# Expert outputs scattered by token inside the expert loop, and the gather-and-combine phase merged into it

## The reference, cut to what matters

```python
top_v, top_i = lax.top_k(logit_e, TOP_K)              # 2 of the 8 experts of the token's group
gate = jax.nn.softmax(top_v, axis=-1) * p_grp
...
def expert_block(args):                               # a block of rows that share an expert
    xb, e = args
    g, u = jnp.split(xb @ w_up[e], 2, axis=-1)
    return (jax.nn.silu(g) * u) @ w_down[e]
...
y = y[dest] * gate.reshape(-1)[order][:, None]
return jax.ops.segment_sum(y, tok_sorted, num_segments=n_tok)
...
x = x + mod[:, 5] * f                                 # then rms_norm_2(x, final_g)
```

## Time and the profile before

| | us |
|---|---|
| median of 3 runs (lowest, highest) | 2867.06 (2861.56, 2873.09) |
| the profiled execution, its own time | 2889.24 |
| its span in the trace | 2887.4 |
| PE busy | 2759.5 (96%) |
| DVE busy | 1506.3 (52%) |
| ACT busy | 777.0 (27%) |
| POOL busy | 79.0 (3%) |
| mean granted clock of PE | 0.982 |

### The profile page before, as it was taken

How to read it: one execution, slowest core, us unless ns; L and a number is a source line. 1 busy time by engine, 2 the same in 40 slices (tenths; PEclk the granted TensorE clock), 3 DMA queues, 4 the chain that set the end, 5 groups by cost and what they waited for, 6 DMA issues and landing times. The chain is left out here.

```text
span 2887.4 us, 44114 instructions
## 1 busy us (share of the span) xinstructions
PE 2759.5 (96%) x18251; PEld 1644.2 (57%) x18251; DVE 1506.3 (52%) x2115; ACT 777.0 (27%) x1444; POOL 79.0 (3%) x106
## 2 busy tenths in 40 slices
PE   8999889999999999999999989999998899999985
PEld 4444554444444444444454445656564899999974
DVE  7886676566666668773642008856765111111103
ACT  2111771111111115412100016756423121112111
POOL 0000000000000000000000000000000000000022
PEclk9999999999999999999999999999999899999997
DMA  3022842111111127763231000022202999999992
GB/s 143 31 73 40 264 175 73 44 44 44 44 44 44 44 67 280 265 245 111 71 90 44 8 11 1 1 59 88 75 7 75 375 402 406 409 410 405 405 359 79
DMA packets 82614, 422.65 MB, mean 146 GB/s; under 512 B 13504, under 2 KB 23232, under 8 KB 66496
## 3 DMA queue, kind: packets, MB, share of 16 engines
q1 hardware_dynamic: 58528, 362.29, 34.1%
q10 hardware_dynamic: 15664, 41.95, 4.0%
q0 software_dynamic: 8304, 16.79, 1.8%
HBM read 393.07 MB, written 51.38 MB: 154 GB/s over the span
## 5 line engine op out<-in xcount | busy, mean ns | idle before, releaser
L3605 PE MATMUL ex_up_ps<-big,ex_xT 128*32 128x128 f32 x3072 | 349.1, 274 | 0.0
L3603 PE MATMUL ex_up_ps<-big,ex_xT 128*32 128x384 f32 x3072 | 344.8, 490 | 0.7 <-ACT ex_xT L3690 0.6
L3605 PEld LDWEIGHTS ex_up_ps<-big,ex_xT 128*32 128x32 f32 x3072 | 334.3, 110 | 0.6
L1758 PE MATMUL ffn_ps<-h,V 128*128 128x512 f32 x504 | 219.7, 592 | 0.0
L2217 PE MATMUL ffn_ps<-big,V 128*128 128x512 f32 x484 | 211.3, 597 | 3.7 <-DVE V L2472 1.4
L3603 PE MATMUL ex_y_ps<-ex_wd,ex_hT 128*32 128x384 f32 x1536 | 180.9, 493 | 5.1 <-issue 4.3
L296 DVE TENSOR_SCALAR_CACHE_REDUCE h<-ad_s_ps 128x1280 f32<-128x1280 f32 x64 | 92.9, 1489 | 172.7 <-PE ad_s_ps L205 172.7
L3605 PE MATMUL ex_y_ps<-ex_wd,ex_hT 128*32 128x128 f32 x1536 | 178.8, 276 | 3.0 <-issue 2.9
L3605 PEld LDWEIGHTS ex_y_ps<-ex_wd,ex_hT 128*32 128x32 f32 x1536 | 169.0, 111 | 7.2 <-issue 6.5
L1758 PEld LDWEIGHTS ffn_ps<-h,V 128*128 128x128 f32 x504 | 95.8, 190 | 120.5 <-issue 120.5
L2217 PEld LDWEIGHTS ffn_ps<-big,V 128*128 128x128 f32 x484 | 92.2, 191 | 120.4 <-issue 114.5
(11 more groups left out here) (603 smaller groups left out, 4799.0 us busy)
## 6 DMA issues: line engine op xcount, KB each, us to landing
big<-in_w_eup SPq DMA_DIRECT2D x64, 2048.0 KB, 20.9
ex_wd<-in_w_edown SPq DMA_DIRECT2D x32, 2048.0 KB, 20.7
V<-in_w_down SPq DMA_DIRECT2D x35, 704.0 KB, 5.6
dn_tail<-in_w_mod ACTq DMA_DIRECT2D x48, 512.0 KB, 5.4
fm_up<-in_w_up SPq DMA_DIRECT2D x22, 1028.0 KB, 4.9
y_dram<-in_cos SPq DMA_DIRECT2D x1, 21504.0 KB, 71.5
y_dram<-big ACTq DMA_DIRECT2D x32, 288.0 KB
dn_tail<-in_w_in SPq DMA_DIRECT2D x17, 512.0 KB, 4.6
```

The costliest lines, as they stand in the source:

```text
L1758: mm = nc.tensor.matmul(bank(i, j), wj[:, k, :], bj[:, k, :], start=(k == 0), stop=(k == 3))
L3603: nc.tensor.matmul(o[32 * g:32 * g + 32, 0:W], rows(g), w[:, 0:W], start=first, stop=last)
L3605: mm = nc.tensor.matmul(o[BR:P, g * P:(g + 1) * P], rows(g), w[:, W:BANK], start=first and g == 0, stop=last and g == GR - 1)
```

## The change

Outputs are no longer stored by block and gathered by token. Each block is scattered to a table of 2048 rows in token order while the loop runs, and read back by plain loads. Of a token's two assignments, the one with the lower expert number goes to row `token`, the other to `1024 + token`; `swapped` remembers where that exchanges the gates.

1. The fill of `y_dram` and its wait are gone.
2. route: `early` and `late` are replaced by one table `rows` (slot to row of the new `y_dram`; an empty slot gets 2048, which is out of bounds and not written). The router adds `swapped` and `code`, and `count` has a third entry. The row ring of h2 stays in SBUF and is used again (`rows`), and `std` with it.
3. experts, ACT: `store_y` becomes `move_y`, three DMAs from SBUF to SBUF that bring the last 256 columns of 32 rows each beside the first 768.
4. experts, POOL: `scatter(i, u)`, an indirect DMA of 96 rows of 4 KB to `y_dram`, and `free(i, u)`, which waits until it has landed and releases the buffer for `keep_y`.
5. the loops are nested, three groups of nine trips, each group with an `If` of its own (not on POOL, whose loop is one of 26 trips).
6. combine is part of experts, with no barrier. DVE computes the gates before its first block. SP loads the lower-expert rows `f0` when pair 15's first block has landed, in the order 4, 0, 5, 1, 6, 2, 7, 3, and the others, `f1`, when the last block has. Tiles 0 to 3 are summed on PE as before; for tiles 4 to 7 ACT scales f0 and DVE adds the residual from the row ring (`added`). The last multiplication of an even tile is split: ACT by the reciprocal root (`leveled`), then GpSimd by the gain. Odd tiles stay on DVE.

```diff
-                sp.dma_start(y_dram.rearrange("(b p) n -> p b n", p=P),
-                             din["cos2"].unsqueeze(1).to_broadcast([P, NB * BR // P, T])).then_inc(y_filled, 16)
...
+                st.done(V_.tensor_tensor(swapped, first_at, c1, ALU.is_gt))
+                for a in range(2):
+                    st.done(V_.tensor_scalar(code[:, a], swapped, float(T) * (1 - 2 * a), float(T) * (a - 2), ALU.mult, ALU.add))
+                    st.done(V_.tensor_tensor(code[:, a], code[:, a], cst["token"], ALU.add))
...
+                for f, got, a in ((f0, got0, 0), (f1, got1, 1)):
+                    sp.wait_ge(up_done, pairs * 2 + (a + 1))
+                    sp.wait_ge(y_free, pairs * 2 + (a + 1))
+                    for t in (4, 0, 5, 1, 6, 2, 7, 3) if a == 0 else range(TT):
+                        sp.dma_start(f[:, t, :], y_dram[a * T + t * P:a * T + (t + 1) * P, :]).then_inc(got[t], 16)
...
+                def free(i, u):
+                    pool.wait_ge(stored[u], i * 16 + 16)
+                    pool.sem_inc(y_free, 1)
+                def scatter(i, u):
+                    nc.gpsimd.tensor_copy(row_at[0:BR, u:u + 1], r["rows"][0:BR, bass.ds(i * 2 + u, 1)]).then_inc(row_set, 1)
...
+                    pool.wait_ge(moved[u], i * (16 * GR) + 16 * GR)
...
+                    pool.indirect_dma_start(y_dram, bass.IndirectOffsetOnAxis(ap=row_at[0:BR, u:u + 1], axis=0), y[0:BR, u, :], None,
+                                            bounds_check=2 * T - 1, oob_is_err=False).then_inc(stored[u], 16)
...
                         pool.wait_ge(turned, i * 2 + 1)
                         gather(i, 1, i * 2)
+                        free(i - 2, 0)
+                        scatter(i - 2, 1)
                         pool.wait_ge(turned, i * 2 + 2)
                         gather(i + 1, 0, i * 2 + 1)
+                        free(i - 2, 1)
+                        scatter(i - 1, 0)
...
+                for t in range(0, TT, 2):
+                    pool.wait_ge(leveled, t // 2 + 1)
+                    nc.gpsimd.tensor_tensor(f1[:, t, :], f1[:, t, :], r["final"], ALU.mult).then_inc(finished[0], 1)
...
+                    for g in range(GR):
+                        act.dma_start(y[32 * g:32 * g + 32, u, 2 * W:D], y[BR:P, u, g * 2 * P:(g + 1) * 2 * P]).then_inc(moved[u], 16)
...
+                with pe.Fori(0, GROUPS) as o:
+                    with pe.If(o * (2 * GROUP) + 2 < nb):
+                        with pe.Fori(0, GROUP) as j:
+                            i = pe.snap(o * GROUP + j + 1)
+                            with pe.If(i * 2 < nb):
...
+                for t in range(PET, TT):
+                    act.wait_ge(got0[t], 16)
+                    nc.scalar.activation(f0[:, t, :], f0[:, t, :], ACT.Copy, scale=r["gate"][:, 0, t:t + 1]).then_inc(scaled, 1)
...
+                    if t % 2:
+                        act.wait_ge(inverted, t)
+                        nc.scalar.activation(f1[:, t - 1, :], f1[:, t - 1, :], ACT.Copy, scale=rms[:, t - 1:t]).then_inc(leveled, 1)
```

More of the change, by code:

```diff
@@ L2673 @@
 NBI = NB + 1
-FAR = 8192
+MIN_NB = -(-2 * T // BR)
+ROWS = 7
+GROUP, GROUPS = 9, 3
 TT = T // P
@@ L3161, in route @@
         g4b, begun = carve(TT, 4), carve(E_)
-        c1, low, pg = (carve(TT) for _ in range(3))
+        c1, low, pg, first_at = (carve(TT) for _ in range(4))
+        code = carve(2, TT)
+        std, swapped = r["std"], r["swapped"]
         base, nblk, incl, onesr, total = (carve(E_) for _ in range(5))
-        bex, cnt, one_bex = carve(1), carve(2), carve(1)
+        bex, cnt, one_bex = carve(1), carve(3), carve(1)
         slotf, blkf, lanef = carve(2, TT), carve(2, TT), carve(2, TT)
@@ L3363, in add_square, with choose @@
                         dve.wait_ge(sum_added, k + 1)
-                def choose(logits, size, onehot, best, tmp):
+                def choose(logits, size, onehot, best, tmp, at=c1):
                     index = cst["index"][:, 0:size].unsqueeze(1).broadcast_to([P, TT, size])
@@ L3461, in _ @@
                                              ALU.is_equal))
-                    st.done(V_.scalar_tensor_tensor(out=here, in0=wide(cst["token"], NB), scalar=-float(T), in1=here,
-                                                    op0=ALU.add, op1=ALU.mult))
+                    st.done(V_.tensor_tensor(here, wide(code[:, a], NB), here, ALU.mult))
                     V_.tensor_tensor(lanes[:, a * TT:(a + 1) * TT, 0:BR], wide(lanef[:, a], BR),
@@ L3520, in experts, with used_pairs @@
             "y_kept"))
+        gates_ready, summed, scaled, added, mixed, squared, rooted, inverted, leveled, step = (ph.sem(x) for x in (
+            "gates_ready", "summed", "scaled", "added", "mixed", "squared", "rooted", "inverted", "leveled", "step"))
+        finished = [ph.sem("finished0"), ph.sem("finished1")]
         def used(eng):
             return eng.value_load(r["count"][0:1, 0:1], min_val=1, max_val=NB)
+        def used_pairs(eng):
+            return eng.value_load(r["count"][0:1, 1:2], min_val=1, max_val=NB // 2)
         with nc.Block() as block:
@@ L3651, in down, with token_sum @@
                     mm.then_inc(y_done, 1)
+                def token_sum(t):
+                    for k in range(KD):
+                        nc.tensor.matmul(sum_ps[t][:, k // 4, k % 4 * P:(k % 4 + 1) * P], h[:, k, t * P:(t + 1) * P], cst["ident"],
+                                         start=(k % 4 == 0), stop=False)
+                    pe.wait_ge(got0[t], 16)
+                    for half in range(2):
+                        mm = nc.tensor.matmul(sum_ps[t][:, half, :], r["diag"][:, t, :], f0[:, t, half * BANK:(half + 1) * BANK],
+                                              start=False, stop=True)
+                    mm.then_inc(summed, 1)
                 turn(0, 0)
@@ new lines, in _ @@
+                for t in range(PET, TT):
+                    dve.wait_ge(scaled, t - PET + 1)
+                    row = rows[:, t % ROWS, :]
+                    nc.vector.scalar_tensor_tensor(out=row, in0=row, scalar=r["std"][:, t:t + 1], in1=f0[:, t, :], op0=ALU.mult,
+                                                   op1=ALU.add).then_inc(added, 1)
+                def mix(t):
+                    if t < PET:
+                        dve.wait_ge(summed, t + 1)
+                        rest = sum_ps[t].rearrange("p a n -> p (a n)")
+                    else:
+                        dve.wait_ge(added, t - PET + 1)
+                        rest = rows[:, t % ROWS, :]
+                    dve.wait_ge(got1[t], 16)
+                    nc.vector.scalar_tensor_tensor(out=f1[:, t, :], in0=f1[:, t, :], scalar=r["gate"][:, 1, t:t + 1], in1=rest,
+                                                   op0=ALU.mult, op1=ALU.add).then_inc(mixed, 1)
@@ L3903, in experts_block @@
         h2_dram = nc.dram_tensor("h2_dram", (T, D), F32).ap()
[L3904 to L3909 removed]
+        y_dram = nc.dram_tensor("y_dram", (2 * T, D), F32).ap()
+        blk, ids, out_rows = keep("blk", [P, NB], I32), keep("ids", [P, NBI], I32), keep("out_rows", [P, NB], I32)
+        count, first_expert = keep("count", [P, 3], I32), keep("first_expert", [P, 1], I32)
+        small = big[:, 20, 4 * P:4 * P + 9 * TT]
+        r = {"g4": small[:, 0:4 * TT].rearrange("p (t g) -> p t g", t=TT), "top": small[:, 4 * TT:5 * TT],
+             "gate": small[:, 5 * TT:7 * TT].rearrange("p (a t) -> p a t", a=2), "std": small[:, 7 * TT:8 * TT], "swapped": small[:, 8 * TT:9 * TT], "rows": out_rows[:], "block": blk[:], "count": count[:], "ids": ids[:], "first": first_expert[:],
+             "gate5": big[:, 18, 0:8 * BR], "final": big[:, 19, :], "diag": big[:, 20, 0:4 * P].rearrange("p (t n) -> p t n", n=P)}
         wu = big[:, 0:16, :].rearrange("p a n -> p (a n)").rearrange("p (u s k n) -> p u s k n", u=2, s=2, k=KD)
```

332 lines of the change are left out of this document (143 added, 189 removed).

## The result

| | median us (lowest, highest) | executions |
|---|---|---|
| before | 2867.42 (2860.70, 2873.09) | 20 |
| after | 2873.11 (2866.05, 2880.86) | 20 |

The ratio is 1.0021, 95% interval 1.0013 to 1.0029: 5.7 us slower, within 0.5%, where I forecast 37 us less. The profiled execution of after took 2877.56, its span is 2875.7.

What follows compares the result with a forecast made beforehand. PE was taken to set the loop's pace, DMA having some 6 us of landing margin. Terms +0.2 - 24.4 - 11.2 - 1.8 = -37.2 us, taken from the 2867.1 median, gave 2830; 8 in 10 range 2816 to 2856.

Steps and rivals of the forecast that it cites:

- router: Before the expert loop: the flag delays the first gather by 0.2 us, other added steps hidden; +0.2 us.
- loop, 30 blocks: Expert loop: net +0.15 us of DMA a block, 4.5 us of later landing, within the margin; 0.
- last period: End of the loop: early gathers gone, four skipped trips instead of twelve; -24.4 us, bounds -5.8 and -26.
- the stall: End of the loop in before: keep_y of block (15,0) starts 18.6 us late, beside POOL's early gathers.
- last keep_y to first mix: After the last block: moves, scatter and f1 loads take 16.5 us instead of 27.7; -11.2 us.
- tail: First f1 mix to the end: multiplications shared with ACT and GpSimd, 25.0 us against 26.8; -1.8 us.
- keep_y(15,0) comes at 2797.4: End of the loop: without early gathers, this block's keep_y comes at its regular period instead of at 2816.00.
- the stall is not recovered: Rival, end of the loop: the 18.6 us belong to profiled executions or software-queue traffic and stay; 2849 us, chance 0.16.
- DMA becomes the bound of the loop: Rival, expert loop: from +0.2 us a block PE waits; 2851 us at a scatter twice the gather; chance 0.08.
- DVE and GpSimd hold each other: Rival, last tiles: four multiplications cost up to 2 us more each, +4 to +8, 2836 us; chance 0.07.
- POOL's chain: Rival, expert loop: scatter landings over 15.9 us delay the next scatter; at 18 us, 2893 us; chance 0.07.
- under 28: Sign in the next profile, expert loop: weight loads land in under 28 us, with a period of 17.0 throughout.

Runs made afterwards that it cites:

- before again: The unchanged kernel before, profiled once more beside before; ratio 0.9997 (0.9985 to 1.0009), span 2870.6 us.
- kernel E: The kernel after with its last multiplication back on DVE for all tiles; 2865.67 us, ratio 0.9987 of before.
- version with two tables: Against kernel E: no moves, output table split into 768 and 256 columns, last columns scattered straight from their partitions; 2858.31 us, ratio 0.9955 of before.

## Why the prediction was wrong

Route starts at 2185.55 in after, at 2185.71 in before again, and at 2175.32 in the first profile of before. The 10 us arise in code that the change doesn't touch, and before again has them as well, so they are no effect of the change. They come in steps: 2.5 us are there by 1340, 7.0 by 1780, the rest later. One step lies where PE's granted clock was 0.50 from 1730 to 1740, against 0.70 and 0.95 in the first profile; the others weren't traced. So I compare after with before again, stage by stage from there:

| step | predicted | measured | how |
|---|---|---|---|
| router | +0.2 | +0.65 | first keep_y 111.97 us behind route's start, was 111.32 |
| loop, 30 blocks | 0 | +5.6 | 516.04 against 510.40 |
| last period | -24.4, of which 18.6 the stall | -5.65 | 11.57 against 17.22 |
| last keep_y to first mix | -11.2 | -2.6 | 16.19 against 18.77 |
| tail | -1.8 | +7.2 | 34.4 against 27.2 |
| sum | -37.2 | +5.3 | the medians differ by 5.7 |

- **The failed step is the gain counted for "keep_y(15,0) comes at 2797.4", and with it for the 27.7 us of the next stretch.** The step itself happens in after, but in before too: both were prices of a gain read from one execution. 18.6 us of the first term and some 10 of the second were not there to be won: in before again and without the early gathers the periods are regular. The rival "the stall is not recovered", held at 0.16, came nearest: the stall belonged to an execution, though not to profiled ones as such, since the second profile lacks it. The bound that the prediction gave its term for that case, -5.8, is what was measured, -5.65. But the rival's price, 2849, was still 24 us low: 8.6 us of the next stretch, 9.0 of the tail and 5.6 of the loop make it up. The prediction had named the sign of the stall, an own time 22.2 us over the median, and subtracted the full gain from the median all the same. With both prices right the sum would have been some -10; the tail and the loop turn that into +5.3. What made that execution slow stays open; it wasn't seen again. (By its own weights the prediction's chances of same and slower are 0.09 and 0.07, not 0.08 and 0.08.)
- **The mechanisms of the end were right, and nearly their durations**: last period 11.57 (forecast 10.1), end of keep_y to first mix 15.2 (16.5). In the second it was luck that the sum came out: the moves took 3.3 us more than reckoned and the scatter 3.9 less. That the shorter last period comes from the skipped trips is shown by the flat loops (18.0 against 12.5).
- **The loop term was mis-sized, in one part.** The prediction had the moves at 0.4 us of DMA a block, and the scatter 0.25 less than the store. The scatter was right: without moves the landings fall by 1.3 us in 5.9 blocks, 0.22 a block. With the moves they grow by some 3.5 us in the same time, 0.6 a block, so the moves cost 0.8. Their own packets take 1.9% of 17 us, 0.32, as priced. The rest seems to be in the loads: 90.8% for 35.82 MB in after against 92.9% for 37.57 MB without moves, so a megabyte of loads takes 2.5% longer, 0.4 us for a block's 6.3 MB. With the moves in halves (90.3% for 36.47 MB) that is nearly gone. But with each block scattered twice it is absent too (87.7% for 35.54 MB), beside the same three moves, so this split is a reading and not shown; the 0.8 itself is read from the landings. Some 0.7 of the 5.6 us are the nest's entry and step. At 0.6 us a block, the 9.6 us from 19.2 to the limit of 28.8 last 16 blocks of the 30, and by 2600 they are gone. "DMA becomes the bound of the loop" was right in kind, with the wrong transfer named: I doubled the scatter in it and not the moves.
- **The tail**: "DVE and GpSimd hold each other" came true at once: three full holds of 2.1 us and their consequences. The tail is 9.4 us over the forecast's 25.0 (I gave 4 to 8, and a chance of 0.07) and 9.1 over kernel E's 25.3. The prediction had read that no run showed the two side by side, and took the row of a lone engine for its value.
- **Fill, nest and router** were right within a microsecond: the fill 0, the nest 0.7 for 0 in the loop and PE silent for 3.19 us for 2.5 behind it, the router 0.65 for 0.2. POOL's chain was no issue in after: scatters land in 9.5 us beside the loads.

The profile's landings were to stay "under 28"; they reached 28.3, and were the sign that told of the loop term in the first profile of after.

Open: why 1 KB rows from SBUF to SBUF slow the loads, and 512-byte rows less. With the same bytes and twice the packets the cost halves, so neither number is the measure; the cause isn't shown. Nor is it shown that 1 KB rows to DRAM are free in the same number: the version with two tables has fewer of them and no bytes more. And what held PE in the first execution of before is open.

## What to carry to other kernels

Price a gain in executions, not in one: when the profiled execution is above the median by as much as the gain, the gain is suspect until a second profile of the unchanged kernel shows it. Where a queue runs at its limit, a surplus of half a microsecond a block adds up over the loop until it meets the buffer's slack, so compute surplus times blocks, with twice the price for transfers that the trace hasn't shown beside the load (0.8 us for 0.4 here). Don't move an elementwise operation from VectorE to GpSimd beside VectorE's own work on SBUF; scatter straight from where the rows lie instead of moving them first (0.9955 of before here, where kernel E has 0.9987).

## What the runs showed of the hardware that was not expected

- Three SBUF to SBUF transfers of 96 KB together, 2% of the DMA engines' time by their own packets (0.32 us a block), cost some 0.8 us a block (landing of the loads 28.3 against 14.0 us). In rows of half the size they cost about half (landing 21.1).
- A one-input VectorE multiplication of 128 x 1024 float32 values takes 0.73 us alone and 2.83 beside GpSimd's; one with an input in PSUM isn't held (1.27).
- Twelve DMA issues in a row hold ScalarE for 7.57 us.
- Twelve skipped trips of a large loop body cost PE 8.7 us; four cost 3.2.

```profile
2815.99 0.90 PE L3637 MATMUL ex_h_ps<-pack,big 128*128 128x128 f32 x3 [8.69 <-issue]
```

```profile
2816.71 0.54 PE L3682 MATMUL ex_ps<-pack,big 128*128 128x128 f32 x3 [3.19 <-issue]
```

The first of these two rows is PE's first work behind the loop in before again, the second in after.
